# First layer's output projection as seven products over two steps of K, four of its eight left-side sums on POOL

## What is computed

```
def conv_gmlp_mixer(xn, w_in, conv_w, ln_g, ln_b, w_s, b_s, w_out):
    proj = xn @ w_in
    ...
    return jnp.concatenate([y_a, y_b], axis=-1) @ w_out      # 512x2048 by 2048x1024
...
    h = x
    for i in range(DEPTH):
        xn = rmsnorm(h, pre_g[i])
        y = conv_gmlp_mixer(...) if i % 2 == 0 else mlstm_mixer(...)
        h = h + rmsnorm(y, post_g[i])
        gate = jax.nn.sigmoid(rmsnorm(h, ple_g[i]) @ w_ple_gate[i])
        h = h + gate * (p[i] @ w_ple[i])
```

## Time and profile before

| | |
|---|---|
| median of 3 runs | 987.69 us (987.11 to 987.70) |
| the profiled execution: its own time | 987.77 us |
| its span in the profile | 985.7 us |
| PE, DVE, ACT, POOL busy, share of the span | 99%, 65%, 51%, 9% |
| matmuls of 512 columns and 128 rows in layer 0's output projection | 384, from 301.1 to 394.4 us |

### The profile page before, as it was taken

One profiled execution on the slowest core, in us unless ns is written; L12 is line 12 of the kernel. 1 busy time (PEld: TensorE's weight loads), 2 busy tenths in 40 slices (PEclk: granted clock), 3 DMA queues, 4 the chain that ended last, 5 costly groups with the idle time before them and its releaser, 6 DMA issues.

```text
span 985.7 us, 12095 instructions
## 1 busy us (share of the span) xinstructions
PE 976.5 (99%) x4534; PEld 805.9 (82%) x4534; DVE 639.3 (65%) x863; ACT 506.6 (51%) x825; POOL 92.6 (9%) x128
## 2 busy tenths in 40 slices
PE   9999999999999999999999999999999999999998
PEld 7888888888877888887888888888888888888887
DVE  6767787786875323849797756775576676421745
ACT  6444545555553333646566656556663775441732
POOL 2020100101000001303010101010101000000400
PEclk9999999999999999999999999999999999999999
DMA  9664946749261432446957647382938163242122
GB/s 334 200 158 144 271 146 178 199 149 251 46 205 70 178 128 86 181 140 143 326 146 197 154 146 180 120 218 86 250 129 214 17 170 134 82 175 86 43 86 85
DMA packets 25482, 154.05 MB, mean 156 GB/s; under 512 B 3153, under 2 KB 4561, under 8 KB 8786
## 3 DMA queue, kind: packets, MB, share of 16 engines
q1 hardware_dynamic: 19090, 107.16, 28.5%
q0 software_dynamic: 6336, 46.14, 24.1%
HBM read 149.09 MB, written 4.19 MB: 156 GB/s over the span
## 4 chain that ended last, share of the span: by engine, by line
PE 93%; DVE 3%; ACT 2%; DMA 1%; issue 1%; DVEq 0%; ACTq 0%
PE bank L2115 17%; PE bank L2118 17%; PE bank L2117 17%; PE bank L2023 9%; PE bank L2025 9%; PE bank L2024 9%; PE bank L2139 1%; PE bank L2141 1%; PE bank L2140 1%; PE bank L2378 1%; DVE w_lo L1357 1%; PE bank L2360 1%; PE bank L2382 1%; ACT w_hi L747 1%; DMA raw<-in_slots 1%
## 5 line engine op out<-in xcount | busy, mean ns | idle before, releaser
L1357 DVE TENSOR_TENSOR w_lo<-raw,w_hi 128x1024 fp32r<-128x1024 f32 x202 | 238.4, 1221 | 139.6 <-ACT w_hi L747 139.0
L2115 PE MATMUL bank<-w_hi,l_hi 128*128 128x512 f32 x784 | 316.7, 404 | 0.8 <-issue 0.7
L2118 PE MATMUL bank<-w_hi,l_lo 128*128 128x512 f32 x784 | 306.0, 390 | 0.0
L2117 PE MATMUL bank<-w_lo,l_hi 128*128 128x512 f32 x784 | 305.5, 390 | 0.0
L747 ACT ACTIVATE w_hi<-raw 128x1024 fp32r<-128x1024 f32 x202 | 202.6, 1054 | 86.0 <-PE bank L2118 43.0
L2115 PEld LDWEIGHTS bank<-w_hi,l_hi 128*128 128x128 f32 x784 | 147.3, 188 | 33.9 <-issue 2.8
L2118 PEld LDWEIGHTS bank<-w_hi,l_lo 128*128 128x128 f32 x784 | 147.1, 188 | 31.3
L2117 PEld LDWEIGHTS bank<-w_lo,l_hi 128*128 128x128 f32 x784 | 147.3, 188 | 30.3 <-issue 1.0
L1322 DVE TENSOR_TENSOR w_lo<-raw,w_hi 128x1024 fp32r<-128x1024 f32 x52 | 61.3, 1220 | 111.2 <-ACT w_hi L700 111.1
L700 ACT ACTIVATE w_hi<-raw 128x1024 fp32r<-128x1024 f32 x52 | 52.3, 1057 | 128.1 <-PE bank L2025 115.7
L2023 PE MATMUL bank<-w_hi,y_hi 128*128 128x512 f32 x224 | 90.6, 404 | 0.2 <-DVE y_lo_end L1541 0.2
(11 more groups left out here) (237 smaller groups left out, 1213.8 us busy)
## 6 DMA issues: line engine op xcount, KB each, us to landing
raw<-in_slots SPq DMA_DIRECT2D x86, 1024.0 KB, 6.8
raw<-in_slots POOLq DMA_DIRECT2D x44, 1024.0 KB, 8.5
h<-in_x SPq DMA_DIRECT2D x8, 512.0 KB, 5.3
out<-h SPq DMA_DIRECT2D x4, 512.0 KB, 8.4
h<-out SPq DMA_DIRECT2D x4, 512.0 KB, 6.8
out<-h SPq DMA_DIRECT2D x7, 256.0 KB, 2.0
raw<-in_slots SPq DMA_DIRECT2D x2, 512.0 KB, 5.8
p_sb<-in_p SPq DMA_DIRECT2D x2, 512.0 KB, 3.8
```

The source lines that it names most:

```text
L1357: dve.tensor_tensor(w7_lo[:, ring(g), c], raw7[:, source(*STEPS[g]), c], w7_hi[:, ring(g), c].bitcast(F32), ALU.subtract).then_inc(w7_lo_r ...
L2115: pe.matmul(dst[:, :], left_hi, w7_hi[:, r, c], start=(first and k == 0), stop=False, skip_group_check=True)
L2117: pe.matmul(dst[:, :], left_hi, w7_lo[:, r, c], start=False, stop=False, skip_group_check=True)
L2118: done = pe.matmul(dst[:, :], left_lo, w7_hi[:, r, c], start=False, stop=(k == 3), skip_group_check=True)
```

## The change

Layer 0's output projection becomes fourteen block products: two steps of K (h = 0, 1; each 1024 of K), and for each the seven products of the scheme. Both steps accumulate in the same banks. The order of the fourteen (called steps 0 to 13 from here on; (h, p) is K step and product) is a table:

```diff
+OUT_ORDER = ((0, 1), (1, 1), (0, 2), (0, 5), (1, 2), (1, 5), (0, 6), (1, 6), (0, 3), (1, 3), (0, 7), (1, 7),
+             (0, 4), (1, 4))
+OUT_LEFTS = ((0, 1), (0, 2), (0, 5), (0, 6), (1, 1), (0, 3), (1, 2), (1, 5), (1, 6), (0, 7), (1, 3), (1, 7),
+             (0, 4), (1, 4))
+OUT_SUMS = ((0, 5), (0, 7), (0, 6), (0, 3), (1, 5), (1, 7), (1, 6), (1, 3))
```

They are steps in the same ring of three as the input projections (`hi7`, `lo7`). The eight blocks of `w_out` are loaded by SP, and ten adding DMAs on POOL make the right-side sums:

```diff
+        def out_fill():
+            u = LAST[0]
+            sp.wait_ge(w7_lo_ready, split_done(u - 1, 4))
+            out_block(0, B21, BX, out_z_in)
...
+            sp.wait_ge(w7_lo_ready, split_done(u, 4))
+            out_block(0, B12, BV, out_v_in)
+            sp.wait_ge(w7_lo_ready, split_done(OUT, 2))
+            out_block(1, B21, BX, out_z_in)
+            sp.wait_ge(w7_lo_ready, split_done(OUT, 5))
+            out_block(0, B22, BV, out_y_in)
+            sp.wait_ge(ybt_ready, 8)
+            for t in range(TILES):
+                sp.dma_start(h[:, t], x[t * P:(t + 1) * P, :]).then_inc(h_in, 16)
...
+            p_load(0)
+            sp.wait_ge(w7_lo_ready, split_done(OUT + 1, 5))
+            out_block(1, B22, BY, out_y_in)
+            sp.wait_ge(w7_lo_ready, split_done(OUT, 7))
+            rows_load(0)
...
+        def out_sums():
+            x, v = (BA, BZ), (BV, BY)
+            out_less(0, 7)
+            out_less(0, 3)
+            pool.wait_ge(out_v_in, 32)
+            for h in range(2):
+                out_add(h, B11, v[h], out_added[5])
+            for h in range(2):
+                pool.wait_ge(w7_lo_ready, split_done(OUT + h, 1))
+                out_add(h, B12, x[h], out_added[6])
+            pool.wait_ge(out_added[6], 32)
+            for h in range(2):
+                out_add(h, B22, x[h], out_added[6])
+            out_less(1, 7)
+            out_less(1, 3)
+            for h in range(2):
+                pool.wait_ge(w7_lo_ready, split_done(OUT + h, 6))
+                out_add(h, B21, x[h], out_added[4])
+            for h in range(2):
+                pool.wait_ge(w7_lo_ready, split_done(OUT + h, 3))
+                out_add(h, B12, v[h], out_s7_in[h])
```

```diff
+            dst, one, two, op = {7: (x2, x1, x2, ALU.subtract), 3: (y1, x1, y1, ALU.add)}[p]
+            pool.tensor_tensor(dst, one, two, op).then_inc(out_sum, 1)
```

PE waits for the results that are copied or subtracted between products:

```diff
+        def out_product(h, p, tp):
...
+                if p in (2, 6):
+                    pe.wait_ge(out_b_copied, tp + 1)
+                if p in (3, 7):
+                    pe.wait_ge(out_c_made, tp + 1)
+                if p == 4:
+                    pe.wait_ge(out_d_made, tp + 1)
```

Token tiles 0 and 1 are finished in banks 0, 1, 4, 5 by step 9. Tiles 2 and 3 are finished in banks 2 and 3 by step 13 (p = 4), and in banks 6 and 7 by `out_d_make` on DVE after step 11 (p = 7). So the residuals of tiles 0 and 1 stand between the last splits, on DVE:

```diff
+            lo7(OUT_STEP + 12)
+            dve.wait_ge(tail_in, 32)
+            dve.wait_ge(h_in, 16 * TILES)
+            dve.wait_ge(w7_lo_ready, split_done(OUT, 4))
+            residual(0, 0)
+            lo7(OUT_STEP + 13)
+            out_d_make(0)
+            residual(0, 1)
+            out_d_make(1)
```

More of the change, by code:

```diff
@@ L157, in tail @@
     def tail(l):
-        for nb in range(2):
+        for nb in range(2 * l):
             for _ in range(3):
@@ L526, in _ @@
         fill(0)
-        tail(0)
+        out_fill()
         load(2)
+        sp.wait_ge(prod_done, 2 * TURN)
+        row(g_pre, g_rows[3:4, :], g_pre_in)
         load(3)
-        sp.wait_ge(y_ready, 16)
-        for t in range(TILES):
-            sp.dma_start(h[:, t], x[t * P:(t + 1) * P, :]).then_inc(h_in, 16)
-        sp.dma_start(g_raw[:, :, :], gif_w).then_inc(gw_in, 16)
-        for s in range(4, 11):
-            load(s)
-        sp.wait_ge(product_ready, N_OUT[0] + 8)
-        row(g_pre, g_rows[3:4, :], g_pre_in)
@@ L687, in _ @@
         head_root(7)
-        tail_norms(1)
+        post(1, 0)
+        post(1, 1)
+        post(1, 2)
+        pre(8)
+        pre(9)
+        post(1, 3)
+        pre(10)
+        pre(11)
     @block.scalar
@@ new lines, in out_steps @@
+        def out_steps():
+            for tp in range(2):
+                wide_tanh(LAST[0], 4, b_of, tp)
+            hi7(OUT_STEP + 2)
+            mixed(4)
+            hi7(OUT_STEP + 3)
+            mixed(5)
+            out_b_copy(0)
+            out_high(0, 3)
+            mixed(6)
+            out_b_copy(1)
+            hi7(OUT_STEP + 4)
+            mixed(7)
+            out_high(1, 2)
+            hi7(OUT_STEP + 5)
+            out_high(1, 5)
+            hi7(OUT_STEP + 6)
+            out_high(1, 6)
+            hi7(OUT_STEP + 7)
+            out_high(0, 7)
+            out_s5_copy(0)
+            out_high(1, 3)
+            out_s5_copy(1)
+            hi7(OUT_STEP + 8)
+            out_high(1, 7)
+            hi7(OUT_STEP + 9)
+            out_high(0, 4)
+            out_square(2, 0)
+            out_square(2, 1)
+            hi7(OUT_STEP + 10)
+            p_high(0)
+            out_high(1, 4)
+            hi7(OUT_STEP + 11)
+            out_square(3, 0)
+            hi7(OUT_STEP + 12)
+            out_square(3, 1)
+            hi7(OUT_STEP + 13)
+            ple_norm(0, 0)
+            out_square(7, 0)
+            hi(0)
+            out_square(7, 1)
+            ple_norm(0, 1)
+            hi(1)
+            out_square(4, 0)
+            out_square(4, 1)
+            ple_copy(0, 0, 0)
+            ple_copy(0, 0, 1)
+            x_high(0, 0)
+            ple_norm(0, 2)
+            ple_copy(0, 1, 0)
+            ple_copy(0, 1, 1)
+            ple_norm(0, 3)
+            ple_copy(0, 0, 2)
+            x_high(1, 1)
+            ple_copy(0, 0, 3)
+            ple_copy(0, 1, 2)
+            x_high(2, 2)
+            ple_copy(0, 1, 3)
+            hi(2)
+            x_high(3, 3)
@@ new lines, in odd_out, with tail @@
+            dve.wait_ge(h_in, 16 * TILES * 2)
+            residual(1, 0)
+            residual(1, 1)
+            residual(1, 2)
+            normalise(8, 0, g_ple)
+            normalise(9, 1, g_ple)
+            residual(1, 3)
+            x_low(4, 0)
+            normalise(10, 2, g_ple)
+            lo(S_PLE[1] + 1)
+            normalise(11, 3, g_ple)
+            x_low(5, 1)
+            x_low(6, 2)
+            lo(S_PLE[1] + 2)
+            x_low(7, 3)
+        def tail(l):
+            if l:
+                odd_out()
+            else:
+                out_steps()
@@ L2120, in product @@
             done.then_inc(prod_done, 1)
+        def out_product(h, p, tp):
+            g = STEP[OUT + h, p]
+            r = ring(g)
+            place = OUT_PLACE[h, p]
+            if tp == 0:
+                pe.wait_ge(y_ready, out_left_count(h, p))
+            if h == 0:
+                if p == 1:
+                    pe.wait_ge(a_free, 2 * LAST[0] + tp + 1)
+                if p == 5:
+                    pe.wait_ge(y32_b, 8)
+                if p in (2, 6):
[4 more added lines that the diff above has]
+                    pe.wait_ge(out_d_made, tp + 1)
+            dst = {1: a_of, 2: a_of, 5: c_of, 3: c_of, 6: b_of, 7: b_of, 4: b_of}[p](tp)
+            first = p in (1, 5) and h == 0
+            tt = slice(tp * P, (tp + 1) * P)
+            for k in range(4):
+                if tp == 0 and k % 2 == 0:
+                    pe.wait_ge(w7_lo_ready, 2 * g + k // 2 + 1)
+                c = slice(k * SEQ, (k + 1) * SEQ)
+                left_hi, left_lo = l_hi[:, place, k, tt], l_lo[:, place, k, tt]
+                pe.matmul(dst[:, :], left_hi, w7_hi[:, r, c], start=(first and k == 0), stop=False,
+                          skip_group_check=True)
+                pe.matmul(dst[:, :], left_hi, w7_lo[:, r, c], start=False, stop=False, skip_group_check=True)
+                done = pe.matmul(dst[:, :], left_lo, w7_hi[:, r, c], start=False, stop=(k == 3),
+                                 skip_group_check=True)
+            done.then_inc(prod_done, 1)
         def plain(p, t):
@@ L2227, in _, with odd_out @@
                 product(u, p, tp)
-        def tail(l):
-            s = S_OUT[l]
+        mix(4)
+        mix(5)
+        for o, (h_of, p) in enumerate(OUT_ORDER):
+            for tp in range(2):
+                out_product(h_of, p, tp)
+                out_piece(2 * o + tp)
+        def odd_out():
+            l = 1
+            s = S_OUT[1]
             for nb in range(2):
```

605 lines of the change are left out of this document (390 added, 215 removed).

## The result

The changed kernel takes **990.18 us** (median of 20 runs, 984.85 to 992.65), the kernel before 987.48 us (median of 20, 986.68 to 988.61). The ratio is 1.0023, 95% interval 1.0016 to 1.0030: slower by a quarter of a per cent, where 979.5 was forecast. The profiled execution took 989.84 us with a span of 988.1; the span before was 985.7.

The account below looks back on a forecast made before the run. PE, busy 99% of the span, was taken as the bound. From 987.8 us, - 10.9 (matmuls) - 0.5 (old wait) + 1.7 (step 12) + 0.7 (tail) + 0.7 (handovers) gave 979.5 us, range 976.3 to 985.5.

Parts of the forecast that it names:

- The 48 matmuls saved: Output projection: 336 matmuls in place of 384, at 0.2267 us each, take 10.9 us off PE.
- the window of the fourteen products: From the end of unit 6 to the first w_ple matmul: 93.3 - 10.9 + 1.2 = 83.6 us.
- The old wait of 0.5 us: PE's wait for a mix, placed in the output projection; claimed to go, saving 0.5 us.
- The rate of the adds: POOL's adding DMAs on the queues: 5.1 us for each 1.05 MB, landing 8.5 us after issue.
- Slow adds, the rival for a slower kernel: Steps 6 and 12: adds become the bound, 1000.5 us at 8.1 us each; chance 0.13, 0.09 beyond 6.6 us.
- adds five and six land at 33: Before step 6: landing 33 us after unit 6, between 30.6 alone and 36.7 always shared with plain loads.
- step 6: Seventh of the fourteen products: starts 37.8 us after unit 6, weights' first half ready at 35.3, no PE wait.
- POOL's sums: Left-side sums, estimated 2.2 us each; rival: one holds DVE before unit 6's last split, giving 981.7 us; chance 0.12.
- The clock: Rival: a wait of 4 us at step 12 lowers the granted clock, 5.4 us more, 988.0 us; chance 0.05.
- Step 12 and the handovers: PE waits 1.0 and 0.7 us for `out_d_make` at step 12; seven engine handovers add 0.7 us.
- Wrong altogether would be a wait in the second layer: Sign that the prediction is wrong: a wait in the second layer, whose work the change leaves as it was.
- the tail: Behind step 13, DVE's residuals and low part against PE's small products: 0.7 us, from nothing to 1.5.

Follow-up runs that it names:

- own_count: Changed kernel with adds five and six counting on two earlier semaphores, and weights of steps 6 and 7 each waiting only for their own add; 981.35 us.
- all_three: Changed kernel with four left-side sums on DVE (second one step later), own add counts for steps 6 and 7, and h loads behind the last plain block; 978.81 us.
- other_sem: Changed kernel with adds five and six counting on two earlier semaphores, weights of steps 6 and 7 still waiting for both adds; 983.01 us.
- held_pair: Changed kernel with add six explicitly held until add five has landed, but step 6's weights waiting for add five alone; 984.25 us.
- The filler: Changed kernel with 16 useless matmuls (3.6 us) in front of step 5's last matmul, in place of PE's wait before step 6; 990.71 us.
- both_h_late: Changed kernel with sums on DVE, own add counts for steps 6 and 7, and loads of h and small arrays behind the last plain block; 979.92 us.
- both: Changed kernel with the four left-side sums on DVE and own add counts for steps 6 and 7 together; 987.41 us, ratio 0.9999.

## Why the prediction was wrong

- **The 48 matmuls saved: right.** In own_count, where nothing waits, the window of the fourteen products is 387.38 - 304.48 = 82.9 us; 93.3 - 10.9 is 82.4. In all_three it is 83.5, with 83.6 forecast, but that closeness is luck: PE waits 0.4 us at step 12 there where 1.7 was forecast, and the 0.5 of the next point, taken off wrongly, makes up for part of it.
- **The old wait of 0.5 us: in the wrong place.** I took it off the output projection, but the mix that waited stands at 281.58, in unit 6. So the window should have been forecast at 84.1.
- **The rate of the adds: near.** From the first landing to the fourth (303.0 to 320.2) it is 17.2 us, and 15.3 were walked, with a hold of 5.4 us before add four inside that I didn't know of. That the fourth lands 15.5 us after the end of unit 6, with 17 forecast, is partly luck, since unit 6 itself ended 3.6 us late. Slow adds, the rival for a slower kernel, aren't what happened.
- **The step that failed: "adds five and six land at 33".** The walk let POOL issue six 0.9 us behind five. It went out 11.2 us later, and landed 39.2 us after the end of unit 6, beyond the 36.7 that I gave as the far bound. That bound priced how long transfers share, and never whether POOL may issue. PE reached step 6 at 38.2 (37.8 forecast), but could start it only at 41.8; the weights had been forecast for 35.3. The tenth add then landed at 67.5 instead of 60.3. other_sem and held_pair each undo one half of this (the hold, the wait for an add that isn't needed), and each takes the wait before step 6 away; own_count does both and is 8.8 us faster.
- **POOL's sums: the size of one was near, its path wrong, the chance too low.** A sum takes 2.4 us (2.2 estimated) and does hold DVE. The rival said 981.7, by a later chain of adds and a longer wait at step 12. What happened is that both sums held DVE (2.2 and 1.8 us), and the loss came at once, as PE's wait for the mix and the low clock behind it: 3.6 us in unit 6. own_count, which has this loss and no wait in the fourteen products, measures 981.35, and all_three, without it, 978.81. That these are close to 981.7 and 979.5 is luck. I gave the rival 0.12 because no row showed DVE stretched. The rule of the Trainium skill, page "SBUF — State Buffer", section "Who interferes with whom", spoke for it; by that rule, which the splits of 4.57 and 4.17 us bear out, the loss was certain and should have been in the sum.
- **The clock: too low a chance, and its place wrong.** I tied it to one wait of 4 us at step 12. It fell behind waits of 2.6 and 3.6 us, in unit 6 and at step 6, and cost 1.5 and 2.5 us in the profiled execution. That the wait of 2.3 us at the program's start left it at 1.00 was no guide to waits in the middle of the work, and not even the same wait of 2.6 us brings it down every time (two of eight executions kept 1.00).
- **Step 12 and the handovers: right in size.** 1.4 + 0.3 against 1.7. That is luck: all that leads there was 7 us late, and PE was late too.
- **"Wrong altogether would be a wait in the second layer".** There is one of 0.3 us (L2740) that wasn't there before, and the one at its start (2.0 us, 1.7 before) was followed by a clock of 0.77 in this execution and 1.00 before.

From 979.5 to 989.84: unit 6 lost 3.6 us. The window is 7.5 over the forecast of 83.6: 3.6 of waiting and 2.5 of clock at step 6, the 0.5 that was taken off in the wrong place, and some 0.9 in small pieces that I did not resolve (0.5 is there in own_count too, where nothing waits). Together 11.1 against 10.3. Outside the window 1.4 us had been set aside, for the tail and the handovers, and 1.05 were lost; and the time outside the span is 0.3 us shorter than before. What stays open is what the low clock alone costs. Of the 20 runs of the changed kernel the eight with a mean clock of 0.996 or more have a median of 988.7, the other twelve of 990.8; that is an association, since a longer wait can lower the clock and lengthen the time. The filler shows that the clock can be held at 1.00 at step 6, but there the chain of adds took the gain away.

## What to carry to other kernels

Adding DMAs from POOL have to be walked in three parts: when the queue can carry them, when POOL may issue them (here the fourth stood until the oldest of the three before it had landed, and with it those that directly followed on its semaphore), and which of them a consumer really needs. Don't put such sums on POOL while DVE is on the way to PE: DVE's next operation stood until the sum was done (2.2 us), and the wait of 2.6 us cost 4 where the clock fell behind it. When a wait is removed and the time does not move, look for the next transfer of the same queues before giving the edit up: the same two edits gave 0.0 us and, with the loads of h moved, 7.6.

## What the runs showed of the hardware

- POOL issued three adding DMAs of 1 MB without a stop (294.99 to 297.92). Before the fourth it was held, and not by the oldest alone: the hold ended when the last add had landed that followed the oldest directly on the same semaphore (add two for add four, five for six, eight for ten; within 0.4 us each time). Adds that had landed still counted: before add six only add five was under way. Add four went out some 13 us behind add two's issue in every kernel here, which is add two's landing. With another semaphore add six went out 11 us sooner and add ten 2.4 us sooner. What inside POOL does this the trace doesn't show, and that it is three belongs to kernels built like these, all with `dynamic_dma_scratch_size=1024` and 1 MB an add; no run varied either.
- The 1 MB load of the last plain block took 6.3 us to land in both_h_late, 14.6 in the changed kernel and 23.6 in `both`. Between the first and the last of these only the loads ahead of it were moved.
- A POOL operation and a DVE operation of 128x1024 held each other: a DVE pair took 4.57 us beside a POOL sum instead of 2.36, and the POOL sum 3.31 instead of 2.40 where DVE's came first.
- The same wait of 2.6 us was followed by a clock of 0.66 to 0.76 in six profiled executions and of 1.00 in two.
- Runs of the kernels with such waits scatter more. The 20 of the changed kernel cover 7.8 us, the 20 of the kernel before 1.9, and the four of all_three 1.4. The four under 988.7 had a mean clock of 0.996 or more, but so had four slower ones, up to 990.4.
